# Rows of the first expert step made on chip by one-hot products, in a two-layer diffusion transformer with a hierarchical mixture of experts

## What is computed

```python
tokens = modulate(h_lat, m[3], m[4]).reshape(B * S, D)
...
g_logits = hf @ wg + bg                      # 4 groups
_, g_sel = lax.top_k(g_logits, 1)
e_logits = (hf @ we + be)...                 # 8 experts in the chosen group
top_p, top_i = lax.top_k(jax.nn.softmax(e_logits, -1), TOP_K)      # 2 of them
weights = p_group * top_p / jnp.sum(top_p, -1, keepdims=True)
expert = g_sel * EXPERTS_PER_GROUP + top_i
...
y = (jax.nn.silu(xb @ w1[e]) * (xb @ w3[e])) @ w2[e]
```

## Time and profile before

| | |
|---|---|
| median of 3 runs | 2463.87 us (2461.8 to 2465.14) |
| the profiled execution's own time | 2463.27 us |
| its span, first to last instruction | 2461.4 us |
| TensorE busy | 2313.6 us (94%), mean granted clock 0.972 |
| VectorE, ScalarE, GpSimd busy | 768.4, 418.8, 280.7 us |
| moved by DMA | 572.28 MB, 232 GB/s in the mean |
| expert products L1091 and L1113 in the chain that ended last | 23% and 11% of the span |
| weight pieces in bigA and bigC | 292 and 92 of 1024 KB, 20.6 and 22.9 us from issue to landing in the median |

### The profile page before, as it was taken

How to read it: one execution, slowest core, us unless ns; L and a number is a source line. 1 busy time by engine, 2 the same in 40 slices (tenths; PEclk the granted TensorE clock), 3 DMA queues, 4 the chain that set the end, 5 groups by cost and what they waited for, 6 DMA issues and landing times.

```text
span 2461.4 us, 28375 instructions
## 1 busy us (share of the span) xinstructions
PE 2313.6 (94%) x10444; PEld 1164.1 (47%) x10444; DVE 768.4 (31%) x1753; ACT 418.8 (17%) x912; POOL 280.7 (11%) x341
## 2 busy tenths in 40 slices
PE   6989999999996999999998999999996999999987
PEld 3546547888554344443333444444553444443332
DVE  3694114555537111111113511111345111111115
ACT  1301233444121101110102200000111101110111
POOL 0000103223122100000000000000232000000000
PEclk9999999999997999999999999999996999999999
DMA  9881000000316999999897210102207999999986
GB/s 386 297 349 58 0 1 1 2 19 19 125 55 257 387 419 414 418 413 409 357 418 278 87 51 26 51 26 88 91 35 298 419 419 416 419 407 410 374 346 256
DMA packets 146797, 572.28 MB, mean 232 GB/s; under 512 B 25033, under 2 KB 50793, under 8 KB 103914
## 3 DMA queue, kind: packets, MB, share of 16 engines
q1 hardware_dynamic: 133418, 536.97, 55.1%
q0 software_dynamic: 13248, 33.57, 3.6%
HBM read 549.51 MB, written 35.65 MB: 238 GB/s over the span
## 4 chain that ended last, share of the span: by engine, by line
PE 81%; DMA 7%; DVE 6%; SPq 2%; issue 2%; POOL 1%; ACT 1%; DVEq 0%; POOLq 0%; ACTq 0%
PE bank L1091 23%; PE bank L1165 13%; PE bank L1113 11%; PE bank L707 8%; PE bank L1014 4%; PE bank L974 4%; PE bank L664 3%; PE bank L810 3%; DVE lnwb L1525 2%; DMA bigA<-in_moe_w 2%; PE bank L1194 2%; SPq L445 2%; PE bank L824 1%; PE bank L793 1%; DMA bigC<-in_moe_w 1%
## 5 line engine op out<-in xcount | busy, mean ns | idle before, releaser
L1091 PE MATMUL bank<-bigA,bigB 128*32 128x512 f32 (+2 forms) x2048 | 524.9, 596 | 0.0
L1165 PE MATMUL bank<-bigB,bigA 128*128 128x512 f32 x768 | 331.6, 595 | 2.0 <-ACT bigB L1244 2.0
L1091 PEld LDWEIGHTS bank<-bigA,bigB 128*32 128x32 f32 (+2 forms) x2048 | 187.1, 141 | 299.1 <-issue 297.0
L707 PE MATMUL bank<-bigC,bigB 128*128 128x512 f32 (+3 forms) x768 | 292.4, 536 | 0.0
L1113 PE MATMUL bank<-bigA,bigB 128*32 128x512 f32 (+2 forms) x992 | 259.2, 612 | 14.8 <-DMA bigA<-in_moe_w 11.8
L1165 PEld LDWEIGHTS bank<-bigB,bigA 128*128 128x128 f32 x768 | 146.5, 191 | 186.6 <-issue 186.6
L707 PEld LDWEIGHTS bank<-bigC,bigB 128*128 128x128 f32 x768 | 142.4, 192 | 127.6 <-issue 119.5
L1244 ACT ACTIVATE bigB<-bank,small 128x128 f32<-128x128 f32 x288 | 107.5, 460 | 381.7 <-PE bank L664 381.7
L1091 PE MATMUL bank<-bigC,bigB 128*32 128x512 f32 (+2 forms) x640 | 163.2, 594 | 0.0
L1113 PEld LDWEIGHTS bank<-bigA,bigB 128*32 128x32 f32 (+2 forms) x992 | 91.4, 143 | 142.3 <-issue 138.2
L2150 POOL DMA_INDIRECT y_rows<-bigB,ints x44 | 44.5, 1011 | 909.0 <-DVE bigB L1936 909.0
(11 more groups left out here) (286 smaller groups left out, 2279.7 us busy)
## 6 DMA issues: line engine op xcount, KB each, us to landing
bigA<-in_moe_w SPq DMA_DIRECT2D x292, 1024.0 KB, 20.6
bigC<-in_moe_w SPq DMA_DIRECT2D x92, 1024.0 KB, 22.9
bigA<-in_ada_w SPq DMA_DIRECT2D x40, 1024.0 KB, 7.4
bigA<-y_rows SPq DMA_DIRECT2D x16, 1024.0 KB, 4.9
bigA<-in_w_in_odd SPq DMA_DIRECT2D x24, 512.0 KB, 6.2
bigA<-in_ada_w SPq DMA_DIRECT2D x4, 2048.0 KB, 12.5
bigC<-in_w_in_even SPq DMA_DIRECT2D x4, 2048.0 KB, 14.3
h_rows<-bigC SPq DMA_DIRECT2D x16, 512.0 KB, 4.8
```

Source lines behind the costliest of these rows:

```text
L707: last = mm(bank(n % 3)[:, 0:w], uT[:, k, t * P:(t + 1) * P], wring[:, g % 2, k, at_:at_ + w], start=(k == 0), stop=(k == KC - 1))
L1091: last = mm(bank(m)[at_:at_ + w, :], xT[:, j, KC // 2 * h + k, at_:at_ + w], w13_at(SLOT_OF[m, h, q][0], k), start=(h == 0 and k == 0), st ...
L1165: last = mm(bank(3 * half + m), wc[:, j, m, k, :], u1T[:, k, half * 512:(half + 1) * 512], start=(k == 0), stop=(k == KC - 1))
```

## The change

The rows of step 0 are no longer gathered. A place's row s of experts 0 and 1 is the token whose rank in that expert is s and that chose it, so the ranks alone say which rows these are. VectorE makes `first_key` (rank + 1 where the token chose expert 0 or 1, else 0) and from it a one-hot `first_is` of 128 tokens x 8 tiles x 128 rows; TensorE multiplies the normed rows `hh` by it, 8 blocks of features by 8 tiles of tokens, 64 products that yield the transposed rows of step 0 in PSUM. ScalarE alone evicts them. The rank products come before the counts' products. Once these products are through, the routing's row of the order is written; the product that spreads the capacities stands after the fifth block. The table's products stand between the two hidden halves of step 0, and the copy of the order before the table's one-hots. Step 0's output follows directly on its own hidden halves, with the transposes of step 1's rows in its middle; from step 1 on the order is as it was. GpSimd gathers steps 1 and 2 first. Piece 12 also waits for the last one-hot product, the wait for a gather moves from piece 14 to piece 16 and is now for the gather of step 1, and the w2 slots of step 0 count as given back one step earlier. Numbers of semaphores and homes of buffers follow. The core of the diff:

```diff
-    return (LAST[q], 2 * m + h) if m < 2 else (LAST[q] + 1, 4)
+    return (LAST[q], 2 * m + h) if m < 2 else (LAST[q] + (LAST[q] > 0), 4)
...
                 if n == PREFETCH:
-                    sp.wait_ge(S("routed"), 6 * l + 4)
+                    sp.wait_ge(S("routed"), 7 * l + 5)
                     sp.wait_ge(S("h_out"), 16 * NT * (l + 1))
-                if n == PREFETCH + 2:
-
-                    sp.wait_ge(S(f"xg_in{l}_0"), 16)
+                    sp.wait_ge(S(f"x_T{l}"), 1)
+                if n == PREFETCH + 4:
+
+                    sp.wait_ge(S(f"xg_in{l}_1"), 16)
...
+                pe.wait_ge(S("routed"), 7 * l + 2)
+                for k in range(KC):
+                    for t in range(NT):
+                        if k == 0:
+                            pe.wait_ge(S("ln"), 2 * l * NT + t + 1)
+                        last = mm(bank(6 + k // 4)[:, (k % 4) * P:(k % 4 + 1) * P], cols(hh[:, t])[:, k, :], first_is[:, t, :],
+                                  start=(t == 0), stop=(t == NT - 1), skip_group_check=True)
+                    if k == 3:
+                        last.then_inc(S("route_mm"), 1)
+                    if k == 4:
+                        pe.wait_ge(S("routed"), 7 * l + 3)
+                        mm(bank(4)[:, 0:3 * NE], cc("ones")[0:NE, :], rows4[:, 0:3 * NE], start=True, stop=True)\
+                            .then_inc(S("route_mm"), 1)
+                last.then_inc(S(f"x_T{l}"), 1)
+                pe.wait_ge(S("routed"), 7 * l + 4)
+                mm(bank(5)[0:1, 0:NE], cc("expert")[0:NE, :], re32[2][0:NE, :], start=True, stop=True, skip_group_check=True)
+                mm(bank(5)[0:1, NE:2 * NE], cc("ones")[0:NE, 0:1], rows4[:, 3 * NE:], start=True, stop=True,
+                   skip_group_check=True).then_inc(S("route_mm"), 1)
+
+                def table():
+
+                    for c in range(16):
+                        pe.wait_ge(S("spot"), l * 16 + c + 1)
+                        last = mm(bank(4)[:, 0:TABLE], lane_is[:, c, :], step_is[:, c, :], start=(c == 0), stop=(c == 15))
+                    last.then_inc(S("route_mm"), 1)
...
+                        if b == 0 and h == 1:
+                            gathered_T(1, 1, 1)
...
-                gathered_T(0, 0, 1)
-                gathered_T(1, 1, 1, 6)
-                for b in range(NB):
+                hidden_half(0, 0)
+                table()
+                hidden_half(0, 1)
+                gated_T(0)
+                output(0)
+                for b in range(1, NB):
                     hidden_half(b, 0)
-                    if b:
+                    if b >= 2:
                         gated_T(b - 1)
                     hidden_half(b, 1)
-                    if b:
-                        gathered_T(b + 1, (b + 1) % 2, (b + 1) // 2 + 1)
+                    gathered_T(b + 1, (b + 1) % 2, (b + 2) // 2)
+                    if b >= 2:
                         output(b - 1)
...
-                rows_T(0, 0)
-                rows_T(1, 1, 6, "u_ev")
-                for b in range(NB):
-                    if b:
-                        act.wait_ge(S(f"g_d{l}"), b)
+                act.wait_ge(S("route_mm"), 8 * l + 5)
+                modulated(parts(xT[:, 0]), 6, mod_of(l, 1), f"xT_ev{l}")
+                act.wait_ge(S(f"x_T{l}"), 1)
+                modulated(parts(xT[:, 0]), 6, mod_of(l, 1), f"xT_ev{l}", 4, KC)
+                silu(0)
+                gated(0)
+                rows_T(1, 1)
...
+                dve.wait_ge(S("route_mm"), 8 * l + 3)
+                rank = bank(2)[:, 0:256].rearrange("p (t e) -> p t e", t=NT)
+                V(v.scalar_tensor_tensor(first_key.rearrange("p (t e) -> p t e", t=NT), rank[:, :, 0:2], 1.0,
+                                         chosen.rearrange("p (t e) -> p t e", t=NT)[:, :, 0:2], ADD, MUL))
+                V.wait()
+                v.tensor_tensor(first_is[:, :, :].rearrange("p t (e s) -> p (t e) s", e=2),
+                                wide(cc("iota")[:, 1:65].unsqueeze(1), [P, 2 * NT, 64]),
+                                wide(first_key.unsqueeze(2), [P, 2 * NT, 64]), ALU.is_equal).then_inc(S("routed"), 1)
+                dve.wait_ge(S("route_mm"), 8 * l + 4)
...
+                dve.wait_ge(S("route_mm"), 8 * l + 7)
+                incl = re32[0]
+                V(v.tensor_copy(incl[0:1, :], bank(5)[0:1, NE:2 * NE]))
+                v.tensor_copy(order[0:1, :], bank(5)[0:1, 0:NE]).then_inc(S("routed"), 1)
                 for c in range(16):
...
-                rows_T(0, 0)
-                rows_T(1, 1, 6, "u_ev_d")
-                for b in range(NB):
-                    if b:
+                gate_up(0)
+                gated(0)
+                rows_T(1, 1)
+                scattered(0)
...
-                gather(0, tok[:, 0:1])
                 gather(1, tok[:, 1:2])
+                gather(0, tok[:, 2:3])
...
                 for b in range(NB):
-                    pool.wait_ge(S(f"x_T{l}"), b + 1)
-                    gather(b % 2, tok[:, b + 2:b + 3])
                     if b:
+                        pool.wait_ge(S(f"x_T{l}"), b + 1)
+                        gather(b % 2, tok[:, b + 2:b + 3])
                         pool.wait_ge(S(f"y_ev{l}"), 2 * b)
```

More of the change, by code:

```diff
@@ L339, in program @@
         rov = at(bigB, 7168, OVER + 1, NE)
-        lane_is = at(bigB, 2048, 16, P)
-        step_is = at(bigB, 6784, 16, TABLE)
+        lane_is = at(bigB, 0, 16, P)
+        step_is = at(bigB, 7392, 16, TABLE)
+        first_key, first_is = bigB[:, 6200:6216], at(bigB, 3072, NT, P)
         slot_f, lane_f, step_f = (at(bigB, 6144 + 16 * n, 16) for n in range(3))
@@ L1046, in moe @@
             def moe(l):
[L1048 to L1051, removed]
+                pe.wait_ge(S("routed"), 7 * l + 1)
                 rank = bank(2)[:, 0:NT * NE]
@@ L1055, in moe @@
                     .then_inc(S("route_mm"), 1)
[L1056 to L1061, removed]
-                   skip_group_check=True).then_inc(S("route_mm"), 1)
@@ L1064, in moe @@
[L1064 to L1067, removed]
+                mm(bank(3)[:, 0:NE], cc("ones"), ahead[:, NT, :], start=True, stop=True, skip_group_check=True)
+                mm(bank(3)[0:NE, NE:NE + 4], ahead[:, NT, :], cc("ones")[:, 0:4], start=True, stop=True,
+                   skip_group_check=True).then_inc(S("route_mm"), 1)
@@ L1077, in hidden_half @@
                     if m == 0:
[L1078 to L1082, removed]
+                        pe.wait_ge(S(f"xT_ev{l}"), 2 * b + 2)
                         if b:
@@ L1134, in block_of @@
                     b = 2 * i + j
-                    pe.wait_ge(S(f"xT_ev{l}"), 2 * b)
+                    pe.wait_ge(S(f"xT_ev{l}"), 2 * b + 2)
                     pe.wait_ge(S(f"silu_a{l}"), b)
@@ L1141, in block_of @@
                         last.then_inc(S(f"h_mm{l}"), 2)
-                    gathered_T(b + 1, 1 - j, i + j + 1)
+                    gathered_T(b + 1, 1 - j, i + 1)
                     gated_T(b)
@@ L1389, in gated @@
                     go(gT[:, 0:2, :].rearrange("p k i -> p (k i)"), bank(4)[:, 0:256], ACT.Copy).then_inc(S(f"gT_ev{l}"), 1)
-                rows_T(0, 0)
-                rows_T(1, 1, 6, "u_ev")
-                for b in range(NB):
-                    if b:
-                        act.wait_ge(S(f"g_d{l}"), b)
+                act.wait_ge(S("route_mm"), 8 * l + 5)
[5 more added lines that the diff above has]
+                rows_T(1, 1)
+                for b in range(1, NB):
+                    act.wait_ge(S(f"g_d{l}"), b)
                     silu(b)
-                    if b:
+                    if b >= 2:
                         gated(b - 1)
-                        rows_T(b + 1, (b + 1) % 2)
+                    rows_T(b + 1, (b + 1) % 2)
                 gated(NB - 1)
@@ L1756, in select @@
                 n = hi - lo
-                dve.wait_ge(S("route_mm"), 7 * l + (1 if lo == 0 else 2))
+                dve.wait_ge(S("route_mm"), 8 * l + (1 if lo == 0 else 2))
                 lt = logit[:, lo:hi]
@@ L1886, in moe @@
                                     ALU.is_equal, MUL).then_inc(S("spot"), 1)
[L1887 to L1890, removed]
                 dve.wait_ge(S("route_a"), l + 1)
@@ L1900, in moe @@
                 V(v.tensor_tensor(wts[:, 1], wts[:, 0], ex, MUL))
-                dve.wait_ge(S("route_mm"), 7 * l + 7)
-                V(v.tensor_scalar(rows_of, bank(1)[:, 0:TABLE], float(ROWS), None, ADD))
+                dve.wait_ge(S("route_mm"), 8 * l + 8)
+                V(v.tensor_scalar(rows_of, bank(4)[:, 0:TABLE], float(ROWS), None, ADD))
                 V.wait()
@@ L2138, in moe @@
             def moe(l):
-                pool.wait_ge(S("routed"), 6 * l + 5)
+                pool.wait_ge(S("routed"), 7 * l + 6)
                 pool.wait_ge(S("h_out"), l * 16 * NT + 16 * NT)
```

14 lines of the change are left out of this document (6 added, 8 removed).

## The result

The kernel after takes **2506.28 us** in the median of 4 runs (2503.43 to 2508.35), beside 2462.84 (2460.5 to 2465.14) for the kernel before in 4 runs. The ratio is 1.0176, 95% interval 1.0158 to 1.0193: 43.4 us slower. The direction was that of the forecast, and so was the wait that does the damage (weights, at step 4 of each layer); the size was not (2481 forecast, range to 2493), because one term of the sum was mis-sized. The profiled execution has a span of 2501.6 us, 40.2 more than before; TensorE is busy for 2364.4 us, 50.8 more, at a mean granted clock of 0.978 instead of 0.972. The rows in this part are of the kernel after.

What follows compares the result with a forecast made beforehand. The prediction took the start of piece 16 to set the time up to step 4 of either layer. Losses of 7.3 and 8.0 us plus 3.0 for stalls made 18.3, so 2481 us; range 2472 to 2493, widened to 2463 to 2493.

Steps and rivals of the forecast that it cites:

- What bounds the kernel: Piece 16 to step 4, either layer: time set by piece 16's start; slack 0.7 us layer 0, none layer 1.
- Ranks and one-hots on VectorE: Routing, before the one-hot products: ranks end at 780.1, small pass 0.2 and comparison 1.22 us, TensorE starts at 781.9.
- The 64 one-hot products: Start of step 0: 128 MATMULs, 24 at 0.227 and 104 at 0.127 us, last one ending at 800.8.
- E: Moment in layer 0 when the last one-hot product ends; forecast 800.8, bounds 798 and 811.
- the bound of 811 for the low clock: End of the one-hot products if the clock stays low throughout: 128 MATMULs at 0.227 us, 29.1 us.
- rival (c): One-hot products stay at the low clock from 781.9 to 811: 38 us more, 2502; chance 0.09.
- TensorE's path: From E: first expert step after 1.7 us, then 43.2 us to step 2, 0.7 us later than before.
- The weight stream: Piece 16 waits for step 1's gather: starts at 820.0 instead of 812.79; stream 8.0 us late with another gather.
- What is late next: Step 4's output waits for weights: layer 0 loses 7.3 us, layer 1 8.0, plus 1.5 per layer for stalls.
- (a): First expert step: the earlier start carries through, 4.7 us per layer, 2454, if piece 16 starts before 812.8; chance 0.13.
- (b): No change: TensorE's path decides at +0.7 us per layer, DMA lateness taken up, 2465; chance 0.10.
- (d): Step 1's gather isn't beside the step but holds piece 16; part of the forecast, no chance of its own.

Runs made afterwards that it cites:

- both: The kernel after with neighbouring columns as stationary operand of the one-hot products and without the gather wait ahead of piece 16: 2463.75 us, ratio 1.0005.
- one-hot stationary: The kernel after with one-hots as stationary operand, normed rows moving, reordered early steps, an early order copy and no gather wait for piece 16: 2462.88 us.
- contiguous kernel: The kernel after with 128 neighbouring columns, not every eighth, as stationary operand of the one-hot products: 2475.09 us, ratio 1.0052.

## Why the prediction was wrong

- **What bounds the kernel**: right. "The time is set by when piece 16 starts" was the claim, and the kernel before with piece 16 held shows it: 10.4 us late in one layer, 19.9 us in all. The slack read from the chain (0.7 us in layer 0, none in layer 1) is borne out from the other side: the two kernels whose TensorE is 2.2 and 3.4 us earlier at step 2 gain nothing that is clear of the noise (1.0004 and 0.9992). One refinement: piece 16 stands for the stream only while there is a hole ahead of it. Where the hole closes, as in "both" and "one-hot stationary", piece 16 goes 8.4 and 5.1 us earlier and the bytes moved up to step 4 are no more than before.
- **Ranks and one-hots on VectorE**: right within 1.0 us (start at 780.89, forecast 781.9). One reading was wrong and cost the sum nothing: VectorE did not pace the 16 table products of the kernel before. Its pairs of one-hots came every 0.41 us (786.90, 787.31, 787.72), a product took 0.44 at a granted clock of 0.50 (7.07 us for 16), and TensorE had no gap between them.
- **The 64 one-hot products**: the step that failed, a term that was mis-sized. The sum had 24 MATMULs at 0.227 and 104 at 0.127 us, 18.9 us with the product put in between; measured 31.4, so that E = 812.3 instead of 800.8, 11.5 us late in each chain behind it. The price of 0.124 to 0.131 came from the earlier trace rows, whose stationary operands are contiguous, and the diff's `cols(hh[:, t])` is not. The operation was counted right and priced from rows of another access pattern. That E came out near the bound of 811 for the low clock is chance: the clock was at its upper level from 785 on, and rival (c), given a chance of 0.09, has nearly the right time (2502) for a wrong reason.
- **TensorE's path**: from E to step 2 46.3 us (812.26 to 858.53), forecast 1.7 + 43.2 = 44.9.
- **The weight stream**: from E to piece 16 18.8 us, forecast 19.2. With the measured E the forecast's own steps give 831.5; it was 831.09.
- **What is late next**: with piece 16 18.3 us late and 0.8 for the third gather, less the slack, 2 x 19.1 - 0.7 = 37.5 us. The rest of the 43.4, 5.9 us, I put down to the stalls behind it (3.0 in the forecast, for both layers); 2.4 of them are seen in layer 0, at the lower clock after the 5.6 us wait, and the others are a difference, not read from rows. TensorE's own account of layer 0 closes: 14.1 us late at step 2, 5.6 of wait, 2.4 of clock make 22.1, and it is 22.0 late at step 6.
- **The sum with only the pace put right** is thus 37.5 + 3.0 = 40.5, 2504, against 2506.28. The contiguous kernel is the case that the forecast had priced: 2481 forecast, 2475.09 measured. There the products started 3.5 us behind the first routing product (forecast 4.0) and the clock rose 4.0 us after that (forecast 5.4), so E lies 20.5 us behind it instead of 22.9, which is 2 x 2.4 of the 5.9 us over both layers.
- **Rivals**: (a) is out: even with piece 16 at 804.2 in "both", ahead of the 812.8 it asked for, nothing was gained. (b) is out for this kernel by 43.4 us and by the new waits for weights; it is what the change comes to with both prices taken off (2463.75). (d), the second gather that holds piece 16, is in the forecast and real: 10.9 us.

## What to carry to other kernels

Before an operation is priced from another row, compare the access patterns of both operands and not only shape and type: here, at the upper clock, 128 columns of float32 that took one number out of 16 or 32 bytes (stationary) or out of 32 (moving) doubled the time, and a stride of 8 bytes cost next to nothing. A wait removed on one engine is worth only what the queue beside it lets through; here the same buffers that fed the new products held back the weight stream, and even at the right pace and without the gather wait the change brings nothing (2463.75). To see whether a stream is late, count the bytes of everything that shares its engines up to a common moment, not the start of one piece.

## What the runs showed that I had not expected

The strided products ran at 0.235 us at a granted clock of 0.51 and at 1.00 alike, so a high clock doesn't say that TensorE is quick; contiguous ones went from 0.22 (18 in 4.0 us) to 0.117. The clock rose at 784.9 in the kernel after, 4.0 us after the products began, while in the kernel before it stayed at 0.50 until 809.6, through 7.07 us of table products without a gap. What makes the difference no run here shows.
